# Product 5 divided once more in the eight convolution groups, x's combinations in turn in one buffer, and a weight sum by load and adding transfer

## The reference

```python
h = rmsnorm(x, norm_g)
b_a, c_a, x_a, z_a, q, k, v, z_b, g_a, g_b = split(h @ w_in)     # 1024 x 12288
y_a = (b_a * conv3(c_a * x_a) * silu(z_a)) @ w_a_out             # gated short convolution
y_b = (rmsnorm(retention(rotary(q), rotary(k), v)) * silu(z_b)) @ w_b_out
x = x + (sigmoid(g_a) * y_a + sigmoid(g_b) * y_b) @ w_o
return rmsnorm(x, final_g)
```

## Time and profile before

| what | value |
|---|---|
| time, median of 3 runs | 1365.60 us (1365.41 to 1365.96) |
| the profiled execution's own time | 1365.87 us |
| its span in the profile | 1364.1 us |
| instructions in the span | 17294 |
| mean granted TensorE clock | 0.998 |
| PE, DVE, ACT, POOL busy | 1351.8, 1060.0, 608.3, 413.7 us |
| HBM read and written | 169.70 and 55.57 MB |

### The profile page before, as it was taken

One profiled execution on the slowest core, in us unless ns is written; L12 is line 12 of the kernel. 1 busy time (PEld: TensorE's weight loads), 2 busy tenths in 40 slices (PEclk: granted clock), 3 DMA queues, 4 the chain that ended last, 5 costly groups with the idle time before them and its releaser, 6 DMA issues.

```text
span 1364.1 us, 17294 instructions
## 1 busy us (share of the span) xinstructions
PE 1351.8 (99%) x6642; PEld 1142.7 (84%) x6642; DVE 1060.0 (78%) x1097; ACT 608.3 (45%) x821; POOL 413.7 (30%) x381
## 2 busy tenths in 40 slices
PE   9999999999999999999999999999999999999997
PEld 7788888888888888888888888888888888888886
DVE  6898465677878777678888778748776998788887
ACT  6843233433333333333333433438778433433445
POOL 0100112344444554444443444315444001100002
PEclk9999999999999999999999999999999999999999
DMA  9646445344433433476666666757768699945443
GB/s 333 216 132 214 141 110 166 95 108 109 109 101 86 108 93 99 136 183 172 176 162 166 147 166 179 223 201 252 267 223 267 141 332 308 235 158 201 162 85 124
DMA packets 112979, 234.81 MB, mean 172 GB/s; under 512 B 7680, under 2 KB 50816, under 8 KB 108032
## 3 DMA queue, kind: packets, MB, share of 16 engines
...
q10 hardware_dynamic: 144, 0.02, 0.0%
HBM read 169.70 MB, written 55.57 MB: 165 GB/s over the span
## 4 chain that ended last, share of the span: by engine, by line
PE 92%; ACT 2%; issue 1%; DVE 1%; DMA 1%; POOL 1%; SPq 1%; POOLq 0%; ACTq 0%; DVEq 0%
PE psum L2625 15%; PE psum L2627 15%; PE psum L2628 15%; PE psum L2768 7%; PE psum L2766 7%; PE psum L2767 7%; PE psum L2549 3%; PE psum L2551 3%; PE psum L2550 3%; PE psum L2538 3%; PE psum L2540 3%; PE psum L2541 3%; PE psum L2670 2%; PE psum L2672 2%; PE psum L2671 2%
## 5 line engine op out<-in xcount | busy, mean ns | idle before, releaser
L1146 ACT ACTIVATE slots<-work 128x1024 fp32r<-128x1024 f32 (+1 forms) x166 | 169.5, 1027 | 418.0 <-PE psum L2628 292.1
L2625 PE MATMUL psum<-hc,slots 128*128 128x512 f32 x912 | 355.0, 389 | 0.0
L2627 PE MATMUL psum<-hc,slots 128*128 128x512 f32 x912 | 354.9, 389 | 0.0
L2628 PE MATMUL psum<-hc,slots 128*128 128x512 f32 x912 | 354.8, 389 | 0.0
L2628 PEld LDWEIGHTS psum<-hc,slots 128*128 128x128 f32 x912 | 171.2, 188 | 35.8
L2625 PEld LDWEIGHTS psum<-hc,slots 128*128 128x128 f32 x912 | 171.2, 188 | 35.3 <-issue 0.4
L2627 PEld LDWEIGHTS psum<-hc,slots 128*128 128x128 f32 x912 | 171.2, 188 | 34.8
L1435 ACT ACTIVATE last_slot<-arena 128x1024 fp32r<-128x1024 f32 x112 | 118.6, 1062 | 163.0 <-PE psum L2768 157.3
L2766 PE MATMUL psum<-last_slot 128*128 128x512 f32 (+1 forms) x452 | 175.3, 388 | 0.0
L2768 PE MATMUL psum<-last_slot 128*128 128x512 f32 (+1 forms) x452 | 175.0, 387 | 0.0
L2767 PE MATMUL psum<-last_slot 128*128 128x512 f32 (+1 forms) x452 | 175.0, 387 | 0.0
...
## 6 DMA issues: line engine op xcount, KB each, us to landing
work<-w_channel SPq DMA_DIRECT2D x80, 512.0 KB, 4.0
work<-w_channel POOLq DMA_DIRECT2D x40, 512.0 KB, 5.5
...
qk<-qk_scratch SPq DMA_DIRECT2D x32, 512.0 KB, 3.4
...
arena<-gate_scratch SPq DMA_DIRECT2D x16, 512.0 KB, 6.8
value_c<-w_value SPq DMA_DIRECT2D x10, 512.0 KB, 4.8
```

The lines of the kernel that those rows point to most:

```text
L1146: nc.scalar.activation(slots[:, u % SLOTS, 0, 0:columns_of(u)], src, ACT.Copy, scale=-1.0 if negated(u) else 1.0).then_inc(w_hi, 1)
L2625: nc.tensor.matmul(bank, slot[:, 0, w], x_high, start=product in STARTS and j == 0, stop=False, skip_group_check=True)
L2627: nc.tensor.matmul(bank, slot[:, 0, w], x_low, start=False, stop=False, skip_group_check=True)
L2628: last = nc.tensor.matmul(bank, slot[:, 1, w], x_high, start=False, stop=j == 3, skip_group_check=True)
```

## The change

- Product 5 of the convolution groups is divided as products 3 and 4 are: units 5a (18 matmuls) and 5b (24) directly behind each other, between product 2 and product 7. Its quarters' products go through banks 1 and 2 of the other set.
- POOL makes four more sums of quarters per convolution group, in the buffer of S1, ahead of those for 3 and 4. DVE gets `second_first`, `second_rest` and one more `low` for product 5, ACT one more `high`.
- `hx` holds the combinations T1, T2, T4 of x for product 5 and for product 4 in turn. Both sets lie in DRAM (`hx_d`), and SP loads T4 (512 KB) and then T1 and T2 (1024 KB) twice in each convolution group: for product 5 once 4b of the former group is done, for product 4 once 5b is done. PE waits for them in each half.
- T3 for product 5 takes the place of its quarter 1 in the convolution groups; DVE and ACT make product 5's combinations in group 0, and SP stores them in DRAM.
- In all groups but the first, S1 is no longer b + d on POOL: SP loads quadrant 3 (d) into buffer e as well, and POOL issues a transfer that adds quadrant 2 (b) to it (`s1`). Buffers d and e keep their roles. S2 waits for this transfer (`s1_in`). The load of d waits for `low` of 4b.

The core of the diff:

```diff
+FIFTHS = CONVS
+LAST_HALF, THIRD_HALF, FIFTH_HALF = 7, 8, 9
+UNIT_TABLE = [(g, p) for g in range(GROUPS) for p in (0, 1, 2, 3, FIFTH_HALF, 4, 5, 6, LAST_HALF, THIRD_HALF)
+              if (p != THIRD_HALF or g in THIRDS) and (p != LAST_HALF or g in TWICE) and (p != FIFTH_HALF or g in FIFTHS)]
 UNITS = VALUE_UNITS + len(UNIT_TABLE)
 
 TILE_ORDER = [(0, 0), (0, 1), (0, 2), (0, 3), (1, 2), (1, 3), (1, 0), (1, 1)]
...
-    return 3 * QUARTER if n in (5, 6) and halved_product(g, product_at(n)) else 2 * HALF
+    return 3 * QUARTER if n in (3, 5, 6) and halved_product(g, product_at(n)) else 2 * HALF
...
-    ROLES.append(dict(a=r["c"], b=r["b"], c=r["a"], d=r["e"], e=r["d"]))
+    ROLES.append(dict(a=r["c"], b=r["b"], c=r["a"], d=r["d"], e=r["e"]))
 LOADED = [{n: 0 for n in range(5)}]
 for r in ROLES:
-    LOADED.append({n: LOADED[-1][n] + (n != r["e"]) for n in range(5)})
...
+        def load_hx(product):
+            n = int(product == 5)
+            sp.dma_start(hx[:, 2].bitcast(F32), hx_d[n, :, 2]).then_inc(t4_in, 16)
+            sp.dma_start(hx[:, 0:2].bitcast(F32), hx_d[n, :, 0:2]).then_inc(t1_t2_in, 16)
...
+            if g in FIFTHS:
+                sp.wait_ge(unit_done, ended_at(g - 1) + 1)
+                load_hx(5)
...
-                sp.wait_ge(w_ready, unit_at(g, 5) + 1)
-                load_work(g + 1, "d", 3)
+                sp.wait_ge(w_ready, fifth_ended_at(g) + 1)
+                load_work(g + 1, "e", 3)
                 sp.wait_ge(w_ready, unit_at(g, 7) + 1)
                 load_work(g + 1, "b", 2)
                 if g in THIRDS and g > THIRDS.start:
                     stores[kind_of(g - 1)](g - 1)
+                if g in FIFTHS:
+                    sp.wait_ge(unit_done, fifth_ended_at(g) + 1)
+                    load_hx(4)
+                if g in THIRDS:
+                    sp.wait_ge(w_ready, ended_at(g) + 1)
+                    load_work(g + 1, "d", 3)
                 sp.wait_ge(w_ready, third_ended_at(g) + 1)
                 load_work(g + 1, "c", 1)
             if g and g not in THIRDS:
                 stores[kind_of(g - 1)](g - 1)
+            if g + 1 < GROUPS and g not in THIRDS:
+                sp.wait_ge(w_ready, ended_at(g) + 1)
+                load_work(g + 1, "d", 3)
             if g == QZS.start:
                 sp.wait_ge(y_out, 16 * len(CONVS))
...
         def s1(g):
-            a, b, c, d, e = buffers(g)
+
+            if g:
+                work_loaded(g, "e")
+                pool.dma_start(work[ROLES[g]["e"]][:, :], w_channel[g, 2], accum_op=ALU.add).then_inc(s1_in, 16)
+            else:
+                a, b, c, d, e = buffers(g)
+                work_loaded(g, "b")
+                work_loaded(g, "d")
+                pool.wait_ge(w_ready, unit_of(1, 3, 1) + 1)
+                nc.gpsimd.tensor_tensor(e, b, d, ALU.add).then_inc(summed, 1)
+
+        def s3(g):
+
             work_loaded(g, "b")
-            work_loaded(g, "d")
-            pool.wait_ge(w_ready, ended_at(g - 1) + 1 if g else unit_of(1, 3, 1) + 1)
-            nc.gpsimd.tensor_tensor(e, b, d, ALU.add).then_inc(summed, 1)
-
-        def s3(g):
-
-            pool.wait_ge(summed, summed_until(g) + 1)
+            if g == 0:
+                pool.wait_ge(summed, summed_until(g) + 1)
             pool.dma_start(work[ROLES[g]["b"]][:, :], w_channel[g, 0], accum_op=ALU.add).then_inc(s3_in, 16)
 
         def s2(g):
             a, b, c, d, e = buffers(g)
+            if g:
+                pool.wait_ge(s1_in, 16 * g)
             pool.wait_ge(w_ready, unit_at(g, 1) + 1)
             nc.gpsimd.tensor_tensor(a, e, a, ALU.add).then_inc(summed, 1)
 
...
-            w = work[ROLES[g]["d" if product == 4 else "a"]]
+            w = work[ROLES[g][{3: "a", 4: "d", 5: "e"}[product]]]
...
+            if g in FIFTHS:
+                second_sums(g, 5)
             if g in THIRDS:
                 second_sums(g, 3)
...
-                if n in (LAST_HALF, THIRD_HALF):
+                if n in (LAST_HALF, THIRD_HALF, FIFTH_HALF):
                     act.wait_ge(summed, second_summed(g, product, 4))
...
+                elif n == 3 and halved_product(g, 5):
+                    second_first(g, 5)
+                elif n == FIFTH_HALF:
+                    second_rest(g, 5, range(1))
+                    low(u + 2)
+                    second_rest(g, 5, range(1, 3))
+                    add(g, 5)
...
+            if product == 5 and g == FIFTHS.start:
+                pe.wait_ge(fifth_kept, 160)
             product_of_quarters(u, 0, quarter(product, 0), psum[:, z, 0:QUARTER], start=True)
             product_of_quarters(u, 1, quarter(product, 2), direct_quarter(g, product, 0))
+            if product != 3 and g in FIFTHS:
+                pe.wait_ge(t4_in, 16 + 16 * hx_loads(g, product))
             product_of_quarters(u, 2, second(product, "T4"), direct_quarter(g, product, 2)).then_inc(unit_done, 1)
 
         def second_half(g, product):
 
-            u, z = (ended_at(g) if product == 4 else third_ended_at(g)), second_bank(g, product)
+            u, z = halved_ended_at(g, product), second_bank(g, product)
             pe.wait_ge(w_ready, u + 1)
+            if product != 3 and g in FIFTHS:
+                pe.wait_ge(t1_t2_in, 16 + 16 * hx_loads(g, product))
             product_of_quarters(u, 2, second(product, "T1"), psum[:, z + 1, 0:QUARTER], start=True)
             product_of_quarters(u, 3, second(product, "T3"), psum[:, z + 1, QUARTER:HALF], start=True)
             product_of_quarters(u, 1, quarter(product, 3), direct_quarter(g, product, 1))
@@ -2590,6 +2710,8 @@
             pe.wait_ge(w_ready, u + 1)
...
                 if halved_product(g, product):
                     first_half(g, product)
+                    if product == 5:
+                        second_half(g, 5)
                     if product == 4:
                         second_half(g, 4)
```

147 lines of the change are left out of this document (103 added, 44 removed).

## The result

| | before | after |
|---|---|---|
| median of 6 runs each | 1365.67 us (1364.67 to 1366.34) | 1374.61 us (1373.25 to 1377.78) |
| ratio, 95% interval | | 1.0066 (1.0055 to 1.0077) |
| forecast | | 1368.5 us, range 1363.6 to 1373.5 |

The kernel became 0.66% slower. The side was forecast, the size was not: 8.9 us instead of 2.9, beyond the range's upper end.

The account below looks back on a forecast made before the run. PE, busy 99%, was taken to bound the kernel. Terms -4.1 (saving), +3.6 (5b's gaps), +1.2 and -0.2 (group 2's gap, product 7's gap), +2.4 (S1's landing) gave +2.9 us: 1368.5 us, range 1363.6 to 1373.5.

Parts of the forecast that it names:

- The saving, -4.1 us: On PE in 8 convolution groups: divided product 5 takes 4.93 us instead of 5.45, 0.52 less per group.
- 5b's gap from the taking of turns, 0.52 us: Groups 3 to 9: DVE's taps and POOL's sums alternate, so 5b's split is late; 7 gaps, +3.6 us.
- my chain: Group 6 ahead of 5b: POOL's sums alternate with DVE's taps; 5b's split ends at 406.19, PE wanted it at 405.76.
- I take 6.1: S1's transfer lands in 6.1 us, making S2 and 5b 0.4 us late in groups 4 to 9; +2.4 us.
- The allowance: Time S1's transfer has from its issue until S2 could start behind product 1's split: some 5.7 us.
- as late as S3 does now: Rival: S1's transfer lands in 6.9 us, total +7.7 us, 1373.3 us; chance 0.10.
- The side, slower: Whole kernel: sum of +2.9 us, median 1368.5 us; chance of slower 0.48, within 0.40, faster 0.12.
- Group 2, +1.0 and -0.52: Group 2: +1.2 us gap ahead of T2, -0.2 for the vanished gap before product 7; product 5 saves 0.52.
- The rest: Added loads, DVE's combinations for product 5 in groups 0 and 1, and later S2 outside the convolution groups cost nothing.
- `hx` in time: Product 4's reloaded T1 and T2 land before 4b needs them, cost nothing; the late-reload rival had +12.5 us, chance 0.08.
- The rival on the other side: Faster: POOL's four sums do not hold up DVE, 5b's split ready at 405.7; -3.1 us, 1362.5; chance 0.12.

Follow-up runs that it names:

- e16: e11 with group 2's low parts of T3 and T1 behind product 7's addition and S3's transfer right behind S1's, as in the change; 1364.13 us, 0.9995 of before.
- e3: The change with x's combinations loaded once, in group 2, and never again (product 4 computed with product 5's); 1366.74 us.
- e14: The change with only product 5's combinations reloaded in each convolution group, product 4's never; 1366.41 us.
- e13: The change with only product 4's combinations reloaded in each convolution group, product 5's loaded in group 2 alone; 1371.58 us.
- e4: The change with SP issuing group 1's gate stores ahead of product 5's first loads in group 2; 1369.22 us.
- e5: The change with SP's loads of d and of product 5's combinations issued only after S1's landing in the convolution groups; 1370.97 us.
- e9: The change with S3's adding transfer issued behind POOL's S2 in the convolution groups alone; 1370.19 us.
- e6: The change with S3's adding transfer issued behind POOL's S2 in all groups; 1376.15 us.
- e2: The change with S1's transfer issued some 3.5 us earlier, between POOL's sums for products 3 and 4, in the convolution groups; 1373.74 us.
- e10: The change with SP's store of y issued behind the 1.5 MB for product 4 instead of ahead; 1372.73 us.
- e12: e11 with the store of y issued behind the 1.5 MB for product 4; 1372.66 us.
- e7: The change with DVE's second tap behind POOL's four sums, the gate's product behind 5b's split and `conv_early` behind `second_first`; 1365.54 us.
- e11: The change with e4, e7 and e9, and in group 2 product 3's later high parts behind 3a's, low parts behind product 5's addition; 1365.48 us.

## Why the prediction was right or wrong

- **The saving, -4.1 us: held.** A divided product 5 without a gap took 4.93 us in e16 (group 4, 328.32 to 333.25), as forecast. The rule that the prediction had weighed, the Trainium skill's "TensorE: Matmul & The Clock Gate", "Back-to-back issue gap", would have given 4.58 for it, and the traces of after show that no more than those of before.
- **5b's gap from the taking of turns, 0.52 us: mechanism right, size too large.** With S1 in time, 5b's first matmul is 0.35 us behind the last one instead of 0.12 and the next 0.1 late as well, some 0.35 together (product 5 takes 5.27 to 5.30 us in most groups of e3 and e14). The third and fourth sum took 1.72 and 1.60 us, where my chain had 1.74 for each.
- **"I take 6.1": the step that failed.** The term for S1's landing was +2.4 us for groups 4 to 9 and measured 8.0 (230.2 us in the change, 222.2 without any reload in e3). S1 landed in 6.9 to 7.8 us. The allowance was somewhat larger than I had (6.24, not 5.7), and still S2 was up to 1.6 us late. I had looked for what follows S1 (the load of d), and took the 1.5 MB for product 4 as done with by then, although I had myself put it at 7.7 to 12.0 us from 407.5: to 415.2 at the earliest and to 419.5 at the latest, with S1 issued at 416.3. I used that estimate only for whether PE would wait for `hx`, and not for what these transfers do to one issued behind them. e13 and e14 name them. The rival "as late as S3 does now" came nearest in time (1373.3), with a landing of 6.9 where it measured 7.5 and nothing about the reload; I gave it 0.10, on two rows, of which the 5.5 was that of a transfer with nothing else beside it.
- **The side, slower: right, with luck.** The forecast had S1 late because of the load of d behind it. In e14 and e3 that load is where the change has it, and S1 lands in 5.7 us, in time. With that and the turns at their measured size the forecast's own terms make -4.1 + 2.5 + 1.0 = -0.6 us. What the profiled execution of the change shows in place of the sum: -4.1 + 2.5 (7 x 0.35) + 3.6 (group 2) + 8.0 (S1) + 0.8 (groups 10 to 18) = 10.8, against 10.7 read from the starts of the groups.
- **Group 2, +1.0 and -0.52: too small by 2.5 us.** The three low parts and `second_first` cost 1.2 as said (e4: 1.19). What I missed is in SP's list: I had counted the new loads in the middle of each group, but not that the first ones go ahead of group 1's stores, which ACT's next instruction waits for. That made it 2.25, and the stretch at the lower clock behind it added 1.6. The prediction had no term for the clock.
- **"The rest": nothing, it was 0.8.** S2 is late in groups 10 to 18 as well, and mostly covered.
- **`hx` in time: right.** PE waited for it nowhere in the change.
- The rival on the other side (sums that do not hold up DVE) is out by the rows of 1.72 and 1.60.

The Trainium skill's "DMA: Bandwidth & Descriptors", "Queues, rings and completion order", says that each transfer engine takes turns between the queue rows that it has work for, a packet at a time. SP's reload and POOL's transfer are of different queues, but in the group looked at above few packets of the two lay side by side, and no run here shows the packets' order on one engine.

**What stays open.** e4, e5, e9 and e13 each have groups whose S1 lands in about 5.6 us and others in which it takes 7.1 or more, with the same order of instructions; e6 and e9 differ only outside the convolution groups. The time that the reload is still under way behind S1's issue goes some of the way. Over groups 3 to 9 of all kernels that have both (without e2, e10 and e12, where other transfers stand beside them), S1 landed within 6.0 us in 35 of 36 groups where the reload landed less than 2.0 us behind S1's issue, and in 9 of 41 where it landed later. With the order of e7 most groups are of the first kind. But e13 has a landing of 5.4 us with 2.7 us beside it, and distances from the reload's issue to S1's are the same 6.0 us in good and bad groups of e5. Nor is the reload the only thing that can do it: in groups 11 to 17, which have no reload, S1 takes 6.6 to 8.1 us in every kernel with this transfer, beside the stores of those groups, mostly without harm to PE. What decides between 5.6 and 7.5 in a single group I did not find; the effect of S3's place is not settled, and that of y's store only by the pair e11 and e12.
